# Routing without SyncE's waits for stores, and routing and experts in one block of the program

## The chip, the cores and the metric

The kernel runs on one core of one Trainium2 chip, in one launch. The metric is device time in microseconds (us): the median of three runs. One further execution was recorded by the hardware profiler, and all rows below come from it. TensorE is written PE, its weight load PEld, VectorE DVE, ScalarE ACT, GpSimd POOL, SyncE SP. A row of the engine "SPq" is a DMA that SP issued.

## The reference, cut to what matters

One decoder layer over 1024 tokens of width 1024, in float32. Attention and pooling come first; the change lies in the two stages after them.

```python
x = x + (sigmoid(g_a) * y_attn + sigmoid(g_p) * y_pool) @ W_o   # called x1 below
h = rmsnorm(x, g_ffn)                                           # called h2 below
logits = h @ w_router + b_router                                # 1024 tokens x 32 experts
top_val, top_idx = lax.top_k(logits, 4)
gates = softmax(top_val)
# tokens sorted by expert, in blocks; each block goes through its expert:
gu = xb @ w_gate_up[e] + b_gate_up[e]
act = (min(up) + 1) * gate * sigmoid(1.702 * gate)
y = act @ w_down[e] + b_down[e]
x = x + sum over a token's 4 experts of gate * y
```

## The kernel before

The program is a row of stages, each a block with one instruction stream per engine: front, attend, merge, route, experts, combine. Between two blocks stands a barrier: an engine that has ended its part of a block waits until all five have.

**Routing** (`route`, L1325 to L1736) makes x1 and h2 for 8 tiles of 128 tokens, numbered n = 0 to 7, in pairs p = 0 to 3 (tiles 2p and 2p + 1). PE multiplies the merged rows by W_o in seven products per pair (L1475, a Strassen scheme; order in `ORDER`), and between these matmuls, at fixed places (`between` in the PE part), does the router work for the pair before: `turn` (eight transposes of h2, L1484), `parts` (router product, L1495), `logits` (L1505) and `ranks` (L1513, L1514). After the last pair come the router steps of tiles 6 and 7 alone, with rows of idle transposes (`stay_warm`, L1518, and L1542). DVE adds the products and the input tile `xt` into `x1[b]`, b = n % 2 (L1611 is the first write into `x1[1]`, in `second_right`; L1638 and L1626 the last ones, for the even and the odd tile, which raise `x1_sum`), scales it to `h2[b]` (L1644, raises `h2_ready`), picks four experts (L1658 to L1665), and turns the ranks into places in the slot list (L1669 to L1688; L1672 raises `base`, for which the next `parts` on PE waits).

POOL makes the sums of input rows that the Strassen scheme needs (L220, four per pair, for the pair ahead), and for each tile writes 4 x 128 token numbers to the slot list in DRAM, by four indirect DMAs of 128 words each (`scatter`, L1403); it waits until they have landed before it goes on. Scatter n runs after DVE has placed tile n. The scatter of the last tile stands in the experts block (L1889). At its end POOL gathers the rows of the first expert item from DRAM (L1435, L1436).

SP issues per tile: the load of input tile n + 2 (L1367), the store of x1 (L1369) and the store of h2 (L1370), 512 KB each. Then it waits until both stores have landed and raises `rows_free`, for which `tile_free` on DVE waits before L1611 (odd tiles) and L1630 (even tiles) overwrite `x1[b]`. Its loop, and what DVE waits for:

```python
if n + 2 < T:
    sp.wait_ge(sem("x1_sum"), n + 1)
    sp.dma_start(xt[b], ...)                       # L1367
sp.wait_ge(sem("h2_ready"), n + 1)
sp.dma_start(x1_dram[rows, :], x1[b])              # L1369
sp.dma_start(h2_dram[rows, :], h2[b])              # L1370
sp.wait_ge(sem("stored"), 32 * n + 32)             # L1371
sp.sem_inc(sem("rows_free"), 1)                    # L1372
...
dve.wait_ge(xt_here[n % 2], 16 * (n // 2 + 1))     # tile_free
dve.wait_ge(sem("rows_free"), n + 1)
```

**Experts** (`experts`, L1750 on) works through items: 160 tokens of one expert, then narrower ones. PE transposes the gathered rows (`turn_x`, L1908, L1912), ACT copies them to SBUF (L2096 to L2099), PE multiplies by the expert's weights (L1927 and others), with DVE and ACT behind it. Before its first item, ACT makes the exponentials of the gates (L2167) and DVE the table of items (from L2402 on), which SP writes out and reads back (L1860, L1862). SP loads 12 MB of weights per item; half of the first item's gate and up weights are loaded at the start of route, the other half by `load_gate_up(sp, 0, 1)` (L1374, issued at L1287) as route's last act on SP, after the gathered rows are there.

Of the kernel before, what the change touches and what calls it, by code (L numbers as in the profile page):

```python
# [20 lines left out]
ALU = mybir.AluOpType  # L21
# [62 lines left out]
def build(nc, x, p, positions, g_mix, w_in, g_q_lat, w_q_b, g_kv_lat, w_kv_b, g_q_head, g_k_nope,  # L84
# [39 lines left out]
    with ExitStack() as top:  # L124
# [1199 lines left out]
        def route():  # L1324
            ctx, sem = stage("route")  # L1325
            with ctx:
                x1 = [view(arena_a, D * (2 + b), D) for b in (0, 1)]
                h2 = [view(arena_a, D * (4 + b), D) for b in (0, 1)]
                junk = view(arena_a, D * 6, D // 2).bitcast(BF16)
                h2T = [view(arena_h, D * (2 + b), K, P) for b in (0, 1)]  # L1330
                zeros = view(arena_h, 4608, SLOTS // P + 2).bitcast(I32)
                ms, rms, rstd = (view(arena_h, 5132 + j, 1) for j in range(3))
                logit = view(arena_h, 5152, E)
                top8 = view(arena_h, 5184, 8)
                idx8 = view(arena_h, 5192, 8).bitcast(U32)
                idxf = [view(arena_h, at, TOP_K) for at in (5200, 7360)]
                onehot = [view(arena_h, at, TOP_K, E) for at in (5248, 7232)]
                taken = view(arena_h, 5376, TOP_K, E)
                slot_e = view(arena_h, 5504, E)
                destf = view(arena_h, 5568, TOP_K)  # L1340
                partT = [view(arena_h, 6912 + P * b, P) for b in (0, 1)]
                fold = view(arena_h, 7168, E)
                QUADS = P // E
                found, place_of, hit = (view(arena_h, 6144 + 2 * P * j, 2 * P) for j in range(3))
                tokc, place, one = (view(arena_h, 4880 + j, 1) for j in range(3))
                earlier = sb("r_earlier", [P, P], BF16, ctx=ctx)
                ones = sb("r_ones", [P, P], BF16, ctx=ctx)
                chosen = [sb(f"r_chosen{b}", [P, E], BF16, ctx=ctx) for b in (0, 1)]
                TB0, TB1, LG, RK = banks[4:8]

                def parts_bank(n):

                    return OUT[1] if n == T - 1 else RK
                with nc.Block() as block:
                    @block.sync
                    def _(sp):
                        sp.wait_ge(sem("zeros"), 1)
                        sp.dma_start(list_dram.rearrange("(p s) o -> p (s o)", p=P), zeros).then_inc(sem("listed"), 16)

                        load_gate_up(sp, 0, 0)  # L1360
                        sp.sem_inc(sem("rows_free"), 2)
                        for n in range(T):
                            b = n % 2
                            rows = slice(tile_of(n) * P, (tile_of(n) + 1) * P)
                            if n + 2 < T:
                                sp.wait_ge(sem("x1_sum"), n + 1)
                                sp.dma_start(xt[b], x2d[tile_of(n + 2) * P:(tile_of(n + 2) + 1) * P, :]).then_inc(xt_here[b], 16)  # L1367
                            sp.wait_ge(sem("h2_ready"), n + 1)
                            sp.dma_start(x1_dram[rows, :], x1[b]).then_inc(sem("stored"), 16)  # L1369
                            sp.dma_start(h2_dram[rows, :], h2[b]).then_inc(sem("stored"), 16)  # L1370
                            sp.wait_ge(sem("stored"), 32 * n + 32)  # L1371
                            sp.sem_inc(sem("rows_free"), 1)  # L1372
                        sp.wait_ge(out_done, 7 * PAIRS)
                        sp.wait_ge(rows_here, 32)  # L1374
                        load_gate_up(sp, 0, 1)

                    @block.gpsimd
                    def _(pool):
                        pool.memset(zeros, 0).then_inc(sem("zeros"), 1)
                        pool.iota(tok, pattern=[[P, T]], base=0, channel_multiplier=1).then_inc(sem("consts"), 1)  # L1380
                        pool.iota(part, pattern=[[1, 1]], base=0, channel_multiplier=1,
                                  allow_small_or_imprecise_dtypes=True).then_inc(sem("consts"), 1)
                        pool.memset(ones[:, :], 1.0).then_inc(sem("consts"), 1)
                        pool.memset(found, 0.0).then_inc(sem("consts"), 1)
                        pool.iota(place_of[:, 0:P], pattern=[[1, P]], base=1, channel_multiplier=0,
                                  allow_small_or_imprecise_dtypes=True).then_inc(sem("consts"), 1)
                        pool.iota(place_of[:, P:2 * P], pattern=[[0, QUARTERS], [1, REST]], base=P + 1, channel_multiplier=0,
                                  allow_small_or_imprecise_dtypes=True).then_inc(sem("consts"), 1)
# [1266 lines left out]
```

## Time and profile before

| | us |
|---|---|
| median of three runs | 2417.8 |
| the three runs | 2417.48, 2417.8, 2420.49 |
| the profiled execution, its own time | 2423.67 |
| span of its trace, first to last instruction | 2422.1 |
| busy in the span: PE / DVE / ACT / POOL | 2371.3 / 1331.2 / 460.3 / 425.9 |
| mean granted TensorE clock | 0.993 |

The trace puts the route block from about 666 us to 808 us after the span's start, and the experts block after it. In rows of a timeline the columns are: start, busy time, engine, line, operation, output and input, count, and in brackets the engine's idle time before it with what ended it. "PEq L1354" and the like is the release of the barrier. Granted clock 1.00 is TensorE's 2.4 GHz, 0.50 is 1.2 GHz.

### The profile page before, as it was taken

The page shows a single profiled execution, that of the slowest core. Times are in us where ns is not written, and L with a number is a line of the kernel's source. Part 1 is how long each engine was busy: PE and PEld are TensorE (multiplying, and loading weights), DVE is VectorE, ACT ScalarE, POOL GpSimd, SP SyncE. Part 2 cuts the span into 40 slices and gives each one's busy share as a digit, 9 for nine tenths or more (in the row PEclk, how much of TensorE's full clock was granted, in tenths as well). Part 3 has the DMA queues.
Part 4 walks back from the last instruction along what each step waited for, and adds up shares of the span by engine and source line. Part 5 has one row for each costly group of instructions (what it writes and reads, how often), then busy time and mean ns, then how long its engine had stood idle before and what let it go on. Part 6 is the DMA issues. An engine that isn't in the chain of part 4 may idle for free. (4 is left out here: it accounts for less than half of the span.)

```text
span 2422.1 us, 45423 instructions
## 1 busy us (share of the span) xinstructions
PE 2371.3 (98%) x15700; PEld 1614.1 (67%) x15700; DVE 1331.2 (55%) x2477; ACT 460.3 (19%) x1150; POOL 425.9 (18%) x589
## 2 busy tenths in 40 slices
PE   8999999999998899999999999999999999999999
PEld 6765664444443888888888888887656565555544
DVE  4665674111255555444544554555767677676565
ACT  3334551000021100001000100000222212121332
POOL 2450102121333211000110110011010101111230
PEclk9999999999998899999999999999999999999999
DMA  4000002311052699887888888888999999999462
GB/s 150 27 18 10 1 0 53 122 29 49 28 176 70 221 377 324 297 294 281 301 294 301 289 308 312 315 301 305 339 329 357 340 345 342 342 347 336 168 200 87
DMA packets 255033, 531.84 MB, mean 220 GB/s; under 512 B 17845, under 2 KB 67909, under 8 KB 254950
## 3 DMA queue, kind: packets, MB, share of 16 engines
q1 hardware_dynamic: 222302, 472.57, 54.9%
q0 software_dynamic: 17440, 38.97, 5.2%
q10 hardware_dynamic: 15208, 19.14, 2.2%
q8 instruction: 58, 0.95, 0.2%
q14 instruction: 25, 0.20, 0.0%
HBM read 498.76 MB, written 31.87 MB: 219 GB/s over the span
## 5 line engine op out<-in xcount | busy, mean ns | idle before, releaser
L1927 PEld LDWEIGHTS banks<-arena_a,arena_w 128*128 128x128 f32 x4608 | 562.9, 190 | 8.1 <-issue 6.5
L1927 PE MATMUL banks<-arena_a,arena_w 128*128 128x144 f32 (+7 forms) x4608 | 566.7, 286 | 1.4 <-ACT arena_a L2099 1.4
L1980 PE MATMUL banks<-arena_w,arena_a 128*64 128x256 f32 x2688 | 298.6, 380 | 3.0 <-DVE arena_a L2258 1.7
L1980 PEld LDWEIGHTS banks<-arena_w,arena_a 128*64 128x64 f32 x2688 | 193.3, 137 | 107.3 <-issue 14.1
L2353 DVE TENSOR_SCALAR arena_m<-banks,arena_m 128x160 f32<-128x160 f32 x144 | 55.2, 383 | 297.1 <-PE banks L1927 296.6
L1305 POOL DMA_DIRECT2D arena_m<-slot_tokens x32 | 18.8, 587 | 1025.7 <-issue 1025.7
L2154 ACT ACTIVATE arena_m<-arena_m 128x160 f32<-128x160 f32 x144 | 48.5, 337 | 785.7 <-DVE arena_m L2353 472.7
L1935 PE MATMUL banks<-arena_w,arena_a 128*64 128x256 f32 x1728 | 197.5, 381 | 0.0
L2036 PE MATMUL banks<-arena_w,arena_a 128*128 128x512 f32 x448 | 194.6, 592 | 0.0
L1935 PEld LDWEIGHTS banks<-arena_w,arena_a 128*64 128x64 f32 x1728 | 120.9, 137 | 67.6 <-issue 10.4
L2036 PEld LDWEIGHTS banks<-arena_w,arena_a 128*128 128x128 f32 x448 | 84.0, 190 | 100.4 <-issue 100.4
L2601 PE MATMUL banks<-arena_h,arena_w 128*128 128x512 f32 (+1 forms) x272 | 111.2, 567 | 0.0
L1129 PE MATMUL banks<-arena_a,arena_w 128*128 128x512 f32 x224 | 97.3, 592 | 0.0
L2601 PEld LDWEIGHTS banks<-arena_h,arena_w 128*128 128x128 f32 x272 | 51.1, 190 | 55.3 <-issue 54.5
L1129 PEld LDWEIGHTS banks<-arena_a,arena_w 128*128 128x128 f32 x224 | 42.6, 190 | 53.6 <-issue 53.6
L285 PE MATMUL banks<-arena_m 96*128 96x512 f32 (+2 forms) x192 | 76.8, 509 | 1.0 <-PEq L366 1.0
L2276 DVE TENSOR_TENSOR arena_w<-arena_w 128x2048 f32<-128x2048 f32 x28 | 64.2, 2292 | 18.9 <-PE banks L1980 17.3
L1104 PE MATMUL banks<-arena_h,arena_w 128*128 128x512 f32 x168 | 74.4, 592 | 0.0
L2279 DVE TENSOR_TENSOR arena_w<-arena_w 128x2048 f32<-128x2048 f32 x28 | 64.2, 2293 | 17.2 <-PE banks L1980 15.0
L293 DVE TENSOR_REDUCE arena_w<-banks 128x1 f32<-128x128 f32 (+3 forms) x64 | 48.4, 757 | 44.3 <-PE banks L288 43.9
L2117 ACT ACTIVATE ex_more<-banks 128x256 f32<-128x256 f32 x28 | 10.8, 384 | 300.5 <-PE banks L1980 300.5
L1307 POOL DMA_DIRECT2D arena_m<-slot_tokens x128 | 66.4, 524 | 3.8 <-issue 3.0
(410 smaller groups left out, 3451.9 us busy)
## 6 DMA issues: line engine op xcount, KB each, us to landing
arena_w<-in_w_gate_up_dram SPq DMA_DIRECT2D x128, 2048.0 KB, 12.7
arena_w<-in_w_down_dram SPq DMA_DIRECT2D x32, 4096.0 KB
expert_rows<-arena_a ACTq DMA_DIRECT2D x104, 128.0 KB, 8.7
arena_a<-in_x_dram SPq DMA_DIRECT2D x16, 512.0 KB, 4.6
arena_w<-in_w_in_dram SPq DMA_DIRECT2D x16, 512.0 KB, 5.4
arena_a<-in_b_down_dram SPq DMA_DIRECT2D x14, 512.0 KB, 15.3
expert_rows<-arena_a ACTq DMA_DIRECT2D x28, 192.0 KB
arena_a<-in_b_down_dram SPq DMA_DIRECT2D x72, 64.0 KB
```

Source lines behind the costliest of these rows:

```text
L285: m = pe.matmul(score[s % 2][j // BANK][:, 0:w], qTh[b][0:HD, s * P:(s + 1) * P], kTh[b][0:HD, j:j + w], start=True, stop=not last, skip_g ...
L1104: m = pe.matmul(bank[:, :], w[:, k, :], src[:, k, :], start=(start and k == 0), stop=(stop and k == KH - 1), skip_group_check=True)
L1129: m = pe.matmul(bank[:, :], w[b][:, k, :], src[:, k, half], start=(k == 0), stop=(k == kk - 1))
L1307: pool.dma_start(idx_b[q * REST:(q + 1) * REST, :], list_dram[bass.ds(slot + P, REST), :]).then_inc(rows_listed, 16)
L1927: m = pe.matmul(GU[f % 3][:, to:to + width], w[c][:, k, at:at + P], xT[:, k, 0:width], start=(k == 0), stop=(k == K - 1), skip_group_check ...
L1935: m = pe.matmul(at[h * TH:(h + 1) * TH, :], x[:, k, :], w[:, k, h * QB:(h + 1) * QB], start=(start and k == 0), stop=(stop and k == KH - 1 ...
L1980: m = pe.matmul(at[h * TH:(h + 1) * TH, :], x[:, k, :], w[:, k, h * QB:(h + 1) * QB], start=(start and k == 0), stop=(stop and k == KH - 1 ...
L2036: return pe.matmul(DN[j][:, :], actT[:, k, 0:P], wd[:, k, halves[j]], start=(k == 0), stop=(k == KF - 1))
L2276: dve.tensor_tensor(b11, b12, b11, ALU.add).then_inc(sem("w_sums"), 1)
L2279: dve.tensor_tensor(b21, b21, b11, ALU.subtract).then_inc(sem("w_sums"), 1)
L2353: dve.tensor_scalar(gc[f % 2], bank[:, 0:WIDTH], bias[:, f:f + 1], SWIGLU_LIMIT, ALU.add, ALU.min).then_inc(sem("gc"), 1)
L2601: m = pe.matmul(gate_into(n, j, part), xnT[n % 2][:, k, :], w_gate[:, k, part], start=(k == 0), stop=(k == K - 1))
```

## The change

SP no longer waits for stores. Each of the two `x1[b]`/`h2[b]` buffers has a semaphore of its own, `stored0` and `stored1`, and DVE waits for it directly. The store of x1 moves from behind `h2_ready` to behind `x1_sum`. `route` and `experts` put their parts into one block; POOL, whose next part begins with the last tile's scatter, gets a wait for that tile's places. The rest of the diff, some 2,000 lines, is indentation; without it:

```diff
-        def route():
-            ctx, sem = stage("route")
-            with ctx:
+        def route(block, ctx, sem):
...
-                with nc.Block() as block:
                     @block.sync
                     def _(sp):
...
                         load_gate_up(sp, 0, 0)
-                        sp.sem_inc(sem("rows_free"), 2)
                         for n in range(T):
                             b = n % 2
                             rows = slice(tile_of(n) * P, (tile_of(n) + 1) * P)
-                            if n + 2 < T:
-                                sp.wait_ge(sem("x1_sum"), n + 1)
+                            sp.wait_ge(sem("x1_sum"), n + 1)
+                            if n + 2 < T:
                                 sp.dma_start(xt[b], x2d[...]).then_inc(xt_here[b], 16)
+                            sp.dma_start(x1_dram[rows, :], x1[b]).then_inc(sem(f"stored{b}"), 16)
                             sp.wait_ge(sem("h2_ready"), n + 1)
-                            sp.dma_start(x1_dram[rows, :], x1[b]).then_inc(sem("stored"), 16)
-                            sp.dma_start(h2_dram[rows, :], h2[b]).then_inc(sem("stored"), 16)
-                            sp.wait_ge(sem("stored"), 32 * n + 32)
-                            sp.sem_inc(sem("rows_free"), 1)
+                            sp.dma_start(h2_dram[rows, :], h2[b]).then_inc(sem(f"stored{b}"), 16)
...
-                        pool.wait_ge(sem("stored"), 32 * T)
+                        pool.wait_ge(sem("stored0"), 32 * (T // 2))
+                        pool.wait_ge(sem("stored1"), 32 * (T // 2))
...
                         def tile_free(n):
                             dve.wait_ge(xt_here[n % 2], 16 * (n // 2 + 1))
-                            dve.wait_ge(sem("rows_free"), n + 1)
+                            if n >= 2:
+                                dve.wait_ge(sem(f"stored{n % 2}"), 32 * (n // 2))
...
-        def experts():
-            ctx, sem = stage("ex")
-            with ctx:
+        def experts(block, ctx, sem, route_sem):
...
-                with nc.Block() as block:
...
                     @block.gpsimd
                     def _(pool):
+                        pool.wait_ge(route_sem("dst"), T)
                         pool.tensor_copy(tokb[1], tok[:, T - 1:T]).then_inc(sem("tokb"), 1)
...
-        route()
-        experts()
+        route_ctx, route_sem = stage("route")
+        experts_ctx, experts_sem = stage("ex")
+        with route_ctx, experts_ctx:
+            with nc.Block() as block:
+                route(block, route_ctx, route_sem)
+                experts(block, experts_ctx, experts_sem, route_sem)
         combine()
```

SP's stream in the routing loop, the turns of tiles 1 and 2, before (the names after "waits" are semaphores; x_rows and h_rows are the x1 and h2 arrays in DRAM):

```order
L1367 DMA arena_a<-in_x_dram 128x1024 [waits route_stored,route_x1_sum]
L1369 DMA x_rows<-arena_a 128x1024 [waits route_h2_ready]
L1370 DMA h_rows<-arena_a 128x1024
L1367 DMA arena_a<-in_x_dram 128x1024 [waits route_stored,route_x1_sum]
L1369 DMA x_rows<-arena_a 128x1024 [waits route_h2_ready]
L1370 DMA h_rows<-arena_a 128x1024
```

And with the change:

```order
L1364 DMA arena_a<-in_x_dram 128x1024 [waits route_x1_sum]
L1365 DMA x_rows<-arena_a 128x1024
L1367 DMA h_rows<-arena_a 128x1024 [waits route_h2_ready]
L1364 DMA arena_a<-in_x_dram 128x1024 [waits route_x1_sum]
L1365 DMA x_rows<-arena_a 128x1024
L1367 DMA h_rows<-arena_a 128x1024 [waits route_h2_ready]
```

The wait for `stored` is gone from SP, and the x1 store stands in front of the wait for `h2_ready`.

POOL's stream where routing ends and experts begin, as one piece of the difference:

```order
-L1435 DMA arena_a<-h_rows,arena_m 128x1024 [waits idx_here,route_stored]
-L1436 DMA arena_a<-h_rows,arena_m 128x256
-L1354 UNCONDITIONAL_BRANCH
-L1884 UNCONDITIONAL_BRANCH [waits barrier_Pool_Activation_PE_DVE_SP_gather]
-L1886 COPY arena_h<-arena_h 128x1
+L1431 DMA arena_a<-h_rows,arena_m 128x1024 [waits idx_here,route_stored1,route_stored0]
+L1432 DMA arena_a<-h_rows,arena_m 128x256
+L1879 UNCONDITIONAL_BRANCH
+L1882 COPY arena_h<-arena_h 128x1 [waits route_dst]
```

The barrier's wait is gone; the copy that starts the last scatter waits for `dst` in its place. On PE, ACT, DVE and SP the same place loses the one branch with its wait for the barrier and nothing else moves.

## Rows read from the trace of the kernel before

**Rows 1.** The page's busy time of PE, with its share of the span
```profile
PE 2371.3 (98%) x15700; PEld 1614.1 (67%) x15700; DVE 1331.2 (55%) x2477; ACT 460.3 (19%) x1150; POOL 425.9 (18%) x589
```

**Rows 2.** Waits of SP, 640 to 850 us: line, releaser, total, times, longest
```profile
SPq L1372 <- DMA h_rows<-arena_a: 33.7, 5, 10.4
```

**Rows 3.** Timeline of PE in route: first matmul of `parts` and of `ranks`, pairs 1 to 3
```profile
698.24 0.64 PE L1495 MATMUL banks<-arena_h 128*32 128x128 f32 x16 [0.17 <-DVE arena_h L1672]
...
705.15 0.18 PE L1513 MATMUL banks<-r_chosen,r_earlier 128*128 128x32 bf16 x1
...
731.55 1.08 PE L1495 MATMUL banks<-arena_h 128*32 128x128 f32 x16 [5.20 <-DVE arena_h L1672]
...
741.47 0.18 PE L1513 MATMUL banks<-r_chosen,r_earlier 128*128 128x32 bf16 x1
...
766.13 1.08 PE L1495 MATMUL banks<-arena_h 128*32 128x128 f32 x16 [3.12 <-DVE arena_h L1672]
...
775.82 0.18 PE L1513 MATMUL banks<-r_chosen,r_earlier 128*128 128x32 bf16 x1
```

**Rows 4.** Timeline of DVE in pairs 2 and 3
```profile
711.17 0.68 DVE L1626 TENSOR_TENSOR arena_a<-banks,arena_a 128x512 f32<-128x512 f32 x1
...
713.59 1.28 DVE L1644 SCALAR_TENSOR_TENSOR arena_a<-arena_a,arena_h,gain_row 128x1024 f32<-128x1024 f32 x1
...
721.14 0.68 DVE L1603 TENSOR_TENSOR arena_a<-banks,arena_a 128x512 f32<-128x512 f32 x1
728.69 0.69 DVE L1611 TENSOR_TENSOR arena_a<-arena_a 128x512 f32<-128x512 f32 x1 [6.87 <-SPq L1372]
...
763.61 0.69 DVE L1611 TENSOR_TENSOR arena_a<-arena_a 128x512 f32<-128x512 f32 x1 [5.34 <-SPq L1372]
```

**Rows 5.** Timeline of the DMAs that SP issues in pairs 2 and 3
```profile
716.80 0.33 SPq L1367 DMA_DIRECT2D arena_a<-in_x_dram  x1
...
717.66 0.43 SPq L1370 DMA_DIRECT2D h_rows<-arena_a  x1
...
752.84 0.33 SPq L1367 DMA_DIRECT2D arena_a<-in_x_dram  x1
```

**Rows 6.** Windows: length, busy time per engine, granted clock, DMA share, GB/s
```profile
724.00:726.00 2.00, 2.00 (x8) 0.72 (x6) 0.00 (x0) 0.00 (x0) 0.00 (x0) 1.00 0.07 10
...
732.00:734.00 2.00, 2.00 (x14) 1.02 (x7) 1.79 (x7) 0.28 (x1) 0.18 (x1) 0.50 0.00 0
```

**Rows 7.** Timeline of POOL: a scatter's first issue, and what followed scatters 1, 3, 4
```profile
715.70 0.98 POOL L1403 DMA_INDIRECT slot_tokens<-arena_h  x1 [0.78 <-POOL arena_h L1399]
...
728.87 1.63 POOL L220 TENSOR_TENSOR arena_h<-arena_m 128x512 f32<-128x512 f32 x1 [8.36 <-DMA slot_tokens<-arena_h]
...
763.44 0.19 POOL L1399 COPY arena_h<-arena_h 128x1 int32<-128x1 int32 x1 [9.12 <-DMA slot_tokens<-arena_h]
...
778.33 0.19 POOL L1399 COPY arena_h<-arena_h 128x1 int32<-128x1 int32 x1 [4.93 <-DMA slot_tokens<-arena_h]
...
794.59 0.99 POOL L1403 DMA_INDIRECT slot_tokens<-arena_h  x1 [0.86 <-DVE arena_h L1688]
```

**Rows 8.** Timeline of all engines where route ends and experts begins
```profile
800.60 7.21 PE L1542 MATMUL banks<-ident 128*128 128x128 f32 x40
...
803.24 0.97 POOL L1436 DMA_INDIRECT arena_a<-h_rows,arena_m  x1 [0.30 <-issue]
807.37 1.01 SPq L1287 DMA_DIRECT2D arena_w<-in_w_gate_up_dram  x2
808.82 1.28 ACT L2167 ACT_TABLE_LOAD   x1 [13.35 <-PEq L1354]
...
809.01 0.41 PE L1908 MATMUL banks<-ident,arena_a 128*128 128x128 f32 x2 [1.20 <-PEq L1354]
```

**Rows 9.** Waits of POOL, 660 to 840 us: line, releaser, total, times, longest
```profile
POOL slot_tokens L1403 <- DVE arena_h L1688: 9.5, 4, 4.9
```

**Rows 10.** All issues of the scatters' line: count, ns shortest, median, longest
```profile
L1403 POOL DMA_INDIRECT slot_tokens<-arena_h x28: 962/972/1948, 702.5 to 798.4; - x28
```

1898 lines of the change are left out of this document (949 added, 949 removed).

## The prediction

> **What bounds the kernel now.** The page first: PE is busy 98% of the span [rows 1], so a change outside PE's work can only win back the rest: idle time of PE, and time in which PE works at the lower clock. The waits of SP show what the change takes away there: 33.7 us in five waits for stores [rows 2]. SP is no bound, so the question is who waits for what SP does late. DVE does. In pair 2 its last sum before the wait ends at 721.14 + 0.68 = 721.82, and L1611 starts at 728.69, 6.87 us later, released by SP's `rows_free`; in pair 3 it waits 5.34 us for the same [rows 4]. And PE waits for DVE: the `parts` of the odd tile needs `base`, which DVE raises 2.9 us after its release (728.69 to 731.55) in pair 2 and 2.5 us after it (763.61 to 766.13) in pair 3. PE stands still 0.17, 5.20 and 3.12 us there in pairs 1, 2 and 3 [rows 3]. After the stall of pair 2 the window from 732 us shows a granted clock of 0.50, that is 1.2 GHz, with PE fully busy [rows 6]. Its price can be read off: from the first `parts` matmul to the first `ranks` matmul PE has the same work in each pair, and takes 705.15 - 698.24 = 6.9 us in pair 1 but 741.47 - 731.55 = 9.9 us in pair 2 and 775.82 - 766.13 = 9.7 us in pair 3 [rows 3]. So each stall costs its own length and about 3 us more. Last I read the place where the blocks meet [rows 8]. No other wait of PE in this stretch is touched by the diff.
>
> **Stores and loads issued earlier.** In pair 2 the stores of tile 3 must land before L1611. Before, the load of tile 5 goes out at 716.80, because SP waits for tile 2's stores, and the h2 store of tile 3 at 717.66 [rows 5]. With the change SP issues the load and the x1 store when `x1_sum` comes, at 711.17 + 0.68 = 711.85, and the h2 store when `h2_ready` comes, at 713.59 + 1.28 = 714.87 [rows 4]: 4.9 us earlier for 1 MB of the three transfers and 2.8 us for the last 0.5 MB. How much earlier they land, no row shows, so I bound it. If the landing moves only as far as the last issue, DVE is released 2.8 us earlier, at 725.9. At the other end it doesn't wait at all, 721.8. Between: the first 1.5 MB (tile 4's load, tile 2's stores) were down when SP went on at 716.80; the next 1.5 MB needed until about 724, when the DMA rate has fallen to 10 GB/s [rows 6], that is some 6.5 us from the issue, of which I estimate 2 us to be start-up that a queue which never runs empty doesn't pay. Following directly on the first part they end near 721, with landing near 722.5. PE was ready at 731.55 - 5.20 = 726.35 and needs DVE released 2.9 us before, by 723.5. I take the middle value, since it rests on how long the same bytes moved: the stall of **5.2 us** goes, and with it the low clock's **3.0 us**.
>
> In pair 3 the load of tile 7 waits in the same way, until 752.84 [rows 5], and the threshold is nearer: PE was ready at 766.13 - 3.12 = 763.01, so DVE must be released by 760.5, 3.1 us earlier than it was. The last issue alone gives 2.8 us of that, the shorter queue the rest. I count the stall, **3.1 us**, and the clock's **2.8 us** as gone, with less confidence. In pair 1 there are only 0.17 us to win. What is late next there is PE's own work: with the stalls gone PE issues its matmuls without a pause until the end of pair 3.
>
> **The first of those to be late after that: POOL.** POOL waits for each scatter's landing. From the last issue's end that took 4.93 us for scatter 4, which runs alone, but 8.36 and 9.12 us for scatters 1 and 3, beside the loads and stores [rows 7]. From 728.87 to the first issue of scatter 6 at 794.59 are 65.7 us. In these POOL waited for DVE up to 9.5 us [rows 9], so its own chain is about 56.2 us, waits for PE's products included, which shrink with the stalls. PE and DVE reach that place 5.2 + 3.0 + 3.1 + 2.8 = 14.1 us sooner, at 780.5. POOL, if scatter 1 lands 2 us sooner than at 728.9, gets there at 726.9 + 56.2 = 783.1 at the latest. That gives back between nothing and 2.6 us; because of the waits still inside the chain I take **1.0 us**. The sums of rows for PE (L220) are not late: they are made a pair ahead, and PE never waited for one here.
>
> **No barrier between the blocks.** SP issues two loads after the gathered rows have landed, at 807.37, for 1.01 us; only then does the barrier open, and PE starts its transposes at 809.01, 1.20 us after its idle transposes ended (800.60 + 7.21 = 807.81) [rows 8]. Now PE waits for the rows alone, which were there before 807.37: **1.2 us**. ACT loads its table at 808.82 for 1.28 us, to 810.10 [rows 8], and only then copies what PE transposed. With no barrier it loads it while it idles (13.35 us before). Bounds: nothing, and 810.10 - 809.01 = 1.1 us; PE needs most of that for the first bank of transposes, so I take **0.3 us**. DVE's table of items starts some 7 us sooner, which pays nothing: PE has the first item's matmuls to do meanwhile, and the table's DMAs stand behind 4 MB of weights in SP's queue. The last scatter moves up behind the gather; it costs nothing, since POOL's next use of the list waits for the table anyway. The cost of `rows_free` and of POOL's new wait for `dst` is nil: both are conditions already true.
>
> One thing speaks against the earlier start of DVE. Issues of scatters take 972 ns in the median and up to 1948 ns [rows 10], the long ones beside DVE work. The Trainium skill says why in "SBUF — State Buffer", section "SBUF: two separate sides": VectorE in its two-port modes locks GpSimd out of their shared port, and descriptors of a GpSimd DMA can't be written meanwhile. By that rule the two gathers, the second issued at 803.24 [rows 8], would now meet DVE's table work, where before DVE idled. From rows alone: two issues lengthened by 0.98 us each is 2.0 us, the high bound; nothing is the low one. DVE's first table operations are as short as routing's, beside which most issues took the median, so I take nothing.
>
> **The sum**: -5.2 - 3.0 - 3.1 - 2.8 + 1.0 - 1.2 - 0.3 = -14.6 us. The experts stage is PE's own work from there on, so it moves up as a whole. Against the profiled execution's 2423.67 us this is 2409.1. The median of the runs lies 5.9 us below that execution; I apply the same difference to it: 2417.8 - 14.6 = **2403.2 us**.
>
> **The rivals.**
> *The stores still land late.* For it: in pair 2 the DMA engines had all but stopped by 724 to 726 us [rows 6], yet DVE was released at 728.69 [rows 4] and POOL, for its scatter, at 728.87 [rows 7]. So the release came with the scatter's last word, not with the stores' data. If that coupling is the limit, only the 2.8 us of the later issue are won in each pair, PE still stalls 2.4 and 0.3 us, and one of the two low-clock stretches stays at most times: -2.8 - 2.8 - 1.5 = -7.1 us with both low clocks kept, 2410.7, and -10.0 with one gone, 2407.8. Against it: the h2 store now enters the queue at 714.87, before scatter 1's first issue at 715.70 [rows 7]. The Trainium skill has such a coupling in "DMA: Bandwidth & Descriptors", section "Queues, rings and completion order": a semaphore's increment lands only after every earlier write of that DMA engine, across its queues. By that rule tile 3's stores escape the scatter if their data get ahead of it, and don't where they queue behind it. The rows of pair 2 agree with it, but no row tells which comes first in the new order. Chance 0.27. In the same band falls the case that the stalls are partly the profiler's, since the plain runs are 5.9 us shorter.
> *The DMA engines are the limit*, and the same bytes land at the same time whatever the issue order. Then only the joint gains: -1.5 us, 2416.3. Against it: 10 GB/s in a window just before the release. Chance 0.12.
> *Slower, by POOL's scatters.* Now loads and stores of two tiles may be queued when a scatter comes, and each scatter's landing takes longer. POOL's chain has four landings before scatter 6, so it grows fourfold; the kernel is slower than before from 726.9 + chain > 794.59 + 1.5, a chain of 69.2 us, that is from 3.3 us more per scatter. The step from alone to beside stores was 9.12 - 4.93 = 4.2 us. With 5 us more on each, scatter 6 starts at 726.9 + 76.2 = 803.1, 8.5 us later than before: 2417.8 + 8.5 - 1.5 = 2424.8. Against it: the bytes are the same and start earlier, so they are more often gone when the scatter comes. Chance 0.06.
>
> **How the numbers follow.** The forecast has 0.55; its own range, from the table load's and the tail's bounds and the clock's, is 2400 to 2406. The range of 8 in 10 takes the late-landing rival in and reaches up to where "same" begins, 2400 to 2413. A measurement of this kernel tells 0.2%, 4.8 us, from no change. Forecast and first rival are faster by more than that (0.82), the second within it (0.12), the third slower (0.06).
>
> **What the profile would show.** Right: no wait of DVE's L1608 (L1611 before) above 2 us; PE's wait before `parts` in pairs 2 and 3 under 0.5 us, and the `parts` to `ranks` stretch 6.9 us in all pairs at clock 1.00; PE's first expert transposes directly behind its idle ones; ACT's table load before the gathered rows land. Wrong: a DVE wait for `stored1` of 3 us or more ending together with POOL's wait for its scatter; or POOL's first issue of scatter 6 waiting for a landing, not for DVE.

## The result, and the profile after

The changed kernel took 2408.5 us (median of five runs, 2406.92 to 2410.38), and the kernel before, run beside it, 2420.5 us: a ratio of 0.995 with a 95% interval of 0.9938 to 0.9961. So it is faster, by 12.0 us. The forecast was 2403.2 us in a range of 2400 to 2413, and 14.6 us to be won. The five runs of before are the three from which the forecast was drawn and two more (2421.43 and 2421.52 us); with these the median is 2.7 us above the 2417.8 of the forecast, and the rest of the miss, 2.6 us, is in the sum. The profiled execution took 2410.38 us (before 2423.67), span 2408.7 us. All shifts below are taken against `ranks` of pair 1, which the change hardly touches (PE's wait in pair 1 was 0.17 us) and which stands 0.37 us later than before (705.52 against 705.15 [rows 3]). Each run has such a small shift of its own; where times of two runs are set against each other below, it is taken off.

PE in route, timeline of the kernel after, the rows that answer to [rows 3] (the line is L1491 now, and L1509 for `ranks`):

```profile
698.62 0.65 PE L1491 MATMUL banks<-arena_h 128*32 128x128 f32 x16
...
705.52 0.18 PE L1509 MATMUL banks<-r_chosen,r_earlier 128*128 128x32 bf16 x1
...
728.13 0.64 PE L1491 MATMUL banks<-arena_h 128*32 128x128 f32 x16 [1.40 <-DVE arena_h L1669]
...
735.04 0.18 PE L1509 MATMUL banks<-r_chosen,r_earlier 128*128 128x32 bf16 x1
...
757.79 0.64 PE L1491 MATMUL banks<-arena_h 128*32 128x128 f32 x16 [1.54 <-DVE arena_h L1669]
...
764.70 0.18 PE L1509 MATMUL banks<-r_chosen,r_earlier 128*128 128x32 bf16 x1
```

The stalls of 5.20 and 3.12 us have shrunk to 1.40 and 1.54, they are not gone. From `parts` to `ranks` it is 6.91 us in both pairs, as in pair 1: the low clock behind each stall is gone whole.

DVE's first write into `x1[1]` (L1608 now), SP's issues of pair 2, and POOL's scatters around them, timelines of the kernel after, for [rows 4], [rows 5] and [rows 7]:

```profile
725.61 0.69 DVE L1608 TENSOR_TENSOR arena_a<-arena_a 128x512 f32<-128x512 f32 x1 [3.61 <-DMA h_rows<-arena_a]
...
755.27 0.69 DVE L1608 TENSOR_TENSOR arena_a<-arena_a 128x512 f32<-128x512 f32 x1 [3.76 <-DMA h_rows<-arena_a]
```
```profile
711.99 0.33 SPq L1364 DMA_DIRECT2D arena_a<-in_x_dram  x1
712.37 0.71 SPq L1365 DMA_DIRECT2D x_rows<-arena_a  x1
715.02 0.32 SPq L1367 DMA_DIRECT2D h_rows<-arena_a  x1
```
```profile
717.02 0.98 POOL L1398 DMA_INDIRECT slot_tokens<-arena_h  x1 [0.78 <-POOL arena_h L1394]
...
728.38 1.27 POOL L220 TENSOR_TENSOR arena_h<-arena_m 128x512 f32<-128x512 f32 x1 [6.54 <-DMA slot_tokens<-arena_h]
...
783.62 0.98 POOL L1398 DMA_INDIRECT slot_tokens<-arena_h  x1 [1.76 <-DVE arena_h L1685]
```

The issues came as early as worked out (load of tile 5 at 711.99, h2 store at 715.02), yet the landing came at 725.6, not 722.5. Windows of the kernel after in that stretch (columns as in [rows 6]):

```profile
718.00:720.00 2.00, 2.00 (x8) 1.00 (x7) 0.30 (x2) 0.28 (x1) 1.39 (x3) 1.00 1.03 422
720.00:722.00 2.00, 2.00 (x11) 1.23 (x10) 1.86 (x8) 0.00 (x0) 1.53 (x2) 1.00 0.47 177
722.00:724.00 2.00, 2.00 (x8) 1.04 (x7) 0.00 (x0) 1.09 (x2) 0.00 (x0) 1.00 0.01 0
```

The DMA engines are full to 720 and empty by about 721, and then DVE waits 4.7 us more for a store whose bytes have gone by. These empty microseconds are what the experiments are about.

The joint, timeline of the kernel after, for [rows 8]:

```profile
784.22 1.28 ACT L2163 ACT_TABLE_LOAD   x1
...
789.34 6.49 PE L1538 MATMUL banks<-ident 128*128 128x128 f32 x40
...
796.65 0.44 PE L1904 MATMUL banks<-ident,arena_a 128*128 128x128 f32 x2 [0.83 <-DMA arena_a<-h_rows,arena_m]
...
798.98 13.31 PE L1923 MATMUL banks<-arena_a,arena_w 128*128 128x160 f32 x96 [1.01 <-ACT arena_a L2095]
```

PE waits for the gathered rows now, not for the barrier, and ACT loads its table 12 us before it is needed.

### The profile page after: what moved, and what is told of

It reads as the page before. It is cut to its first block and busy times, and to the rows that moved or that the text cites. A ratio compares the mean times of both kernels' runs of the same rounds, so it can differ in the third digit from the quotient of the medians.

```text
span 2408.7 us, 45402 instructions
## 1 busy us (share of the span) xinstructions
PE 2364.5 (98%) x15700; PEld 1611.2 (67%) x15700; DVE 1334.0 (55%) x2477; ACT 460.3 (19%) x1150; POOL 423.7 (18%) x589
```

## The experiments

Two theories for what is left of DVE's wait. **Coupling**: a store's completion is held up while list writes (POOL's scatter, 512 writes of 4 bytes per tile) are in flight. **Bytes**: the loads and stores just take that long. Each kernel ran five to eleven times, on chips on which before took 2424 to 2426 us, so only the ratios are compared; "ratio" is to the kernel before on the same chip, with its 95% interval. Diffs are against the changed kernel unless said.

**Each half of the change alone.** First SP's half in the two blocks of before (diff against the kernel before):

```diff
+                            sp.dma_start(x1_dram[rows, :], x1[b]).then_inc(sem(f"stored{b}"), 16)
                             sp.wait_ge(sem("h2_ready"), n + 1)
...
-                            sp.wait_ge(sem("stored"), 32 * n + 32)
-                            sp.sem_inc(sem("rows_free"), 1)
...
-                            dve.wait_ge(sem("rows_free"), n + 1)
+                            if n >= 2:
+                                dve.wait_ge(sem(f"stored{n % 2}"), 32 * (n // 2))
```

> The change's SP edit alone, route and experts as two blocks with the barrier between them. Theory (two parts that add up, as the change's profile reads: the stalls and the low clock in pairs 2 and 3 give some 11.4 us, the missing barrier some 1.4 us): 1.4 us slower than the change, ratio to the kernel before about 0.9957; PE waits 1.4 and 1.5 us before parts of tiles 3 and 5, no window at clock 0.50 between 730 and 772 us, PE's first expert transposes again behind a barrier release. Rival (the parts depend on each other, since the barrier hid or took over what the stalls cost): over 4 us slower than the change.

Measured: ratio 0.9966 (0.9954 to 0.9978), 2414.3 against 2424.3 us. DVE waits 4.29 and 4.42 us, PE 2.07 and 2.20, and there is no low clock behind them. By the ratio it is 3.9 us slower than the change, where 1.4 was expected. The barrier's cost is there as before, and here more than its wait: a stretch of low clock follows (in the kernel before the clock is full there), and the first item's matmuls take 36.72 us, in the change 35.04 (timeline of PE, then a window):

```profile
789.39 6.55 PE L1540 MATMUL banks<-ident 128*128 128x128 f32 x40
797.31 0.41 PE L1907 MATMUL banks<-ident,arena_a 128*128 128x128 f32 x2 [1.37 <-PEq L1354]
...
799.94 36.72 PE L1926 MATMUL banks<-arena_a,arena_w 128*128 128x160 f32 x256 [1.35 <-ACT arena_a L2098]
```
```profile
801.00:803.00 2.00, 2.00 (x10) 2.00 (x9) 1.93 (x4) 0.19 (x1) 1.70 (x2) 0.50 1.05 392
```

Then the one block with SP's part as it was:

```diff
-                    sp.wait_ge(sem("x1_sum"), n + 1)
                     if n + 2 < T:
+                        sp.wait_ge(sem("x1_sum"), n + 1)
...
+                    sp.wait_ge(sem("stored"), 32 * n + 32)
+                    sp.sem_inc(sem("rows_free"), 1)
```

> One block for route and experts, SP's waits for stores and rows_free as before. Theory of two parts that add up: 1.4 us faster than before, ratio about 0.9994; PE still waits about 5.2 and 3.1 us before parts of tiles 3 and 5 and works at clock 0.50 for 6.8 us after each; its expert transposes follow the idle ones as in the change. Rival (DVE's early start on the item table and the last scatter, moved behind the gathers, make the gathered rows land later, so the joint is worth nothing): within 0.3 us of before, with PE's wait for the gathered rows over 2 us.

Measured: ratio 0.9986 (0.9977 to 0.9995), 2421.6 us. PE stands still 5.55 and 4.28 us, and the low clock follows both times:

```profile
731.00:733.00 2.00, 2.00 (x10) 0.84 (x3) 1.82 (x8) 0.28 (x1) 0.00 (x0) 0.50 0.00 0
767.00:769.00 2.00, 2.00 (x4) 0.72 (x3) 0.31 (x3) 0.00 (x0) 1.10 (x2) 0.50 0.00 0
```

(windows of this run). The two halves, 0.34% and 0.14%, add up to the change's 0.5% within their intervals, and SP's half is the larger. The intervals reach 2 to 3 us to each side, so these times leave room for an interplay of a microsecond or two, such as the low clock behind the barrier in e1.

**List writes taken away beside the stores.** This kernel leaves out the list writes of tiles 1 and 3 (`SKIP` is 1, 3), so those tiles' tokens are missing from the slot list; all else runs:

```diff
-                    for j in range(TOP_K):
+                    for j in range(0 if n in SKIP else TOP_K):
```

> The change, with the list writes (four indirect DMAs each) of tiles 1 and 3 left out; those tokens' entries in the slot list stay zero, so their experts' rows are token 0's. Amount of work elsewhere is the same. Theory A (the stores' semaphores are held by the scatter's writes to DRAM): DVE's waits at L1608 in pairs 2 and 3 fall from 3.6 and 3.8 us to under 0.5, PE's 1.4 and 1.5 us to nothing, 2.9 us faster than the change. Theory B (the bytes of two tiles' loads and stores set the landing, at some 400 GB/s): DVE's waits stay between 3 and 4 us and the time within 0.5 us of the change.

Measured: ratio 0.9924 (0.991 to 0.9937), 2405.5 us. Timelines of DVE and PE, and two windows:

```profile
720.86 0.69 DVE L1609 TENSOR_TENSOR arena_a<-arena_a 128x512 f32<-128x512 f32 x1 [0.66 <-DMA h_rows<-arena_a]
```
```profile
718.00:720.00 2.00, 2.00 (x9) 1.04 (x8) 1.83 (x9) 0.00 (x0) 0.00 (x0) 1.00 0.80 326
720.00:722.00 2.00, 2.00 (x9) 1.11 (x8) 0.90 (x2) 1.09 (x2) 0.00 (x0) 1.00 0.03 10
```

The same store, the same bytes before it: the engines run empty at about 719.6 (0.80 of the first window), and DVE goes on at 720.9, 1.3 us after that; in the change it was 725.6 - 720.9 = 4.7 us (0.47 of the window from 720). On the change's scale, 1.8 us later (`ranks` of pair 1 at 703.74 here), the landing would be 722.6. DVE waits 0.66 us instead of 3.61. PE has no wait before `parts` at all. Coupling holds; bytes are excluded as the cause of 3 of these 4.7 us. Pair 3 shows the same: in the change the engines run empty at about 750.5 and DVE goes on at 755.27, again 4.7 us later, and without the list writes DVE doesn't wait there. Since tokens are missing, the ratio of this kernel is no gain to be had. The Trainium skill's rule in "DMA: Bandwidth & Descriptors", section "Queues, rings and completion order", is that the semaphore's increment lands only after every earlier write of that DMA engine, whatever its queue; this trace agrees.

**The list writes held instead of left out.** A first try named the wrong count, and POOL waited for stores that had landed long before:

```diff
+                    if n in (1, 3):
+                        pool.wait_ge(sem("stored1"), 16 * (n + 1))
```

> The change, with the list writes of tiles 1 and 3 held back on POOL until both stores of that tile have landed. Coupling theory: with no list write in flight the stores land at about 721 us, as they did where the list writes were left out, DVE's waits at L1608 are under 1 us in both pairs and PE's at parts nothing (2.9 us won), while POOL's chain grows by some 2 to 4 us per hold and gives that back at the gathers: about the change's time, up to 3 us slower. Bytes theory: DVE's waits stay at 3.6 us and POOL's holds come on top.

Measured: ratio 0.9947 (0.9933 to 0.996), DVE waits 4.11 and 3.20 us, PE 1.88 and 0.98. It held nothing, so it is a second measurement of the change, and shows how far two traces of one kernel differ: half a microsecond in each of these waits, and 0.6 us at the first expert matmul. With the count of the stores meant:

```diff
-                        pool.wait_ge(sem("stored1"), 16 * (n + 1))
+                        pool.wait_ge(sem("stored1"), 16 * (n + 3))
```

> The hold of the run before was put on stores that had landed 20 us earlier: scatter 1 runs beside tile 3's stores, not tile 1's. Here the list writes of tile 1 wait until tile 3's stores have landed, those of tile 3 until tile 5's have; nothing is left out. Coupling theory: DVE's waits at its first write into x1[1] fall from 3.6 and 3.8 us to under 1 us, as without those list writes, and PE's waits at parts vanish; POOL's chain grows by about 4 us per hold (scatter 1 from 717 to 721 us, after that list writes with no stores beside them), so the gathers come 2 to 6 us later and the whole is 0 to 4 us slower than the change. Bytes theory: DVE's waits stay at 3.6 us.

Measured: ratio 0.9972 (0.9961 to 0.9983), 2418.0 us. Timelines of POOL, DVE and PE:

```profile
720.73 1.06 POOL L1400 DMA_INDIRECT slot_tokens<-arena_h  x1 [6.26 <-DMA h_rows<-arena_a]
...
788.25 0.98 POOL L1400 DMA_INDIRECT slot_tokens<-arena_h  x1 [0.78 <-POOL arena_h L1394]
```
```profile
751.83 1.31 DVE L1610 TENSOR_TENSOR arena_a<-arena_a 128x512 f32<-128x512 f32 x1 [2.54 <-DMA h_rows<-arena_a]
```
```profile
800.53 0.56 PE L1906 MATMUL banks<-ident,arena_a 128*128 128x128 f32 x2 [4.65 <-DMA arena_a<-h_rows,arena_m]
```

With no list write in flight the stores of tile 3, the last of them issued at 713.24, land by 720.7, and in pair 2 DVE doesn't wait. In pair 3 it does, for 2.54 us, where under 1 was expected. The hold had pushed scatter 2 among the next transfers: its four issues went out from 736.07 to 741.83, the loads and stores of tiles 4 and 5 from 736.71 to 743.37. In that stretch the DMA engines were busy and moved little (window of this run):

```profile
742.00:744.00 2.00, 2.00 (x6) 0.75 (x4) 1.30 (x2) 1.28 (x3) 0.00 (x0) 1.00 1.24 162
```

They ran empty at about 750.8, and DVE went on 1.1 us after that, so this wait was for late data and not for a late completion. The rest of the time is lost behind: POOL's chain is some 6 us late, scatter 6 starts at 788.25 and waits for a landing, PE waits 4.65 us for the gathered rows, and with the low clock behind that wait the first item's matmuls take 36.87 us instead of 35.04. By the ratios the kernel is 5.3 us slower than the change; 0 to 4 was expected. That is the slower rival's mechanism, made by hand.

**The x1 store's place.** Behind `h2_ready`, as before:

```diff
-                    sp.dma_start(x1_dram[rows, :], x1[b])...
                     sp.wait_ge(sem("h2_ready"), n + 1)
+                    sp.dma_start(x1_dram[rows, :], x1[b])...
```

> The change with the x1 store moved back behind the wait for h2_ready. Coupling theory (what counts is which store data get ahead of the list writes): two stores, not one, now go out at 715.0 us, 2 us before scatter 1's first issue, so the h2 store is further back in the queue and DVE's waits grow by up to 1 us, PE's with them: 0 to 2 us slower than the change. Rival (the early x1 store is what the gain came from): the waits return to 5 us and more and a window at clock 0.50 follows, over 5 us slower than the change.

Measured: ratio 0.9942 (0.9928 to 0.9956). DVE waits 3.61 and 4.91 us, PE 1.43 and 2.69. The times show no difference from the change, so the earlier x1 store is not where the bulk of the gain came from. The one trace shows some: a low clock follows the stall of 2.69 us, and the first expert matmul comes 2.5 us later than in the change, more than the 0.6 us by which two traces of the change differ.

**DVE waits only for what it overwrites.** L1608 writes `x1`, not `h2`, so a semaphore for each store lets it start when the x1 store alone has landed; the wait for the h2 store moves to where `h2[b]` is written:

```diff
-                        dve.wait_ge(sem(f"stored{n % 2}"), 32 * (n // 2))
+                        dve.wait_ge(sem(f"x1_out{n % 2}"), 16 * (n // 2))
...
+                    if n >= 2:
+                        dve.wait_ge(sem(f"h2_out{n % 2}"), 16 * (n // 2))
```

> The change, with x1's and h2's stores on semaphores of their own: DVE waits for x1's store before it overwrites x1, and for h2's store only before it overwrites h2, some 20 us later. Both theories let the x1 store, issued 4.6 us before the first list write of scatter 1, land before DVE wants it at 722 us: DVE's waits at its first write into x1[1] under 0.5 us, PE's 1.4 and 1.5 us gone, 2.9 us faster than the change, ratio to before about 0.9939. Rival (x1's semaphore too is held by scatter 0's or 1's writes, or the wait turns up at h2's scaling): a DVE wait of 2 us or more at one of the two places, and less than 1 us gained.

Measured: ratio 0.995 (0.9937 to 0.9964), 2411.8 us: no gain over the change (0.9939 was expected), though in pairs 2 and 3 neither DVE nor PE waits at these places any more. Timelines of POOL and PE:

```profile
781.48 0.26 POOL L1394 COPY arena_h<-arena_h 128x1 int32<-128x1 int32 x1 [4.96 <-DMA slot_tokens<-arena_h]
782.52 0.99 POOL L1398 DMA_INDIRECT slot_tokens<-arena_h  x1 [0.78 <-POOL arena_h L1394]
```
```profile
783.15 7.24 PE L1538 MATMUL banks<-ident 128*128 128x128 f32 x40
795.10 0.44 PE L1906 MATMUL banks<-ident,arena_a 128*128 128x128 f32 x2 [4.71 <-DMA arena_a<-h_rows,arena_m]
798.13 37.07 PE L1925 MATMUL banks<-arena_a,arena_w 128*128 128x160 f32 x256 [0.96 <-ACT arena_a L2097]
```

What was won in route is waited away at its end: POOL is the late one there now, and behind the 4.71 us the clock falls to 0.50 (window 797 to 800), so the first item's matmuls take 37.07 us where they take 35.04 in the change.

**Gather first.** The scatter of tile 6 moved behind the two gathers, with and without the split semaphores:

```diff
-                scatter(T - 2, last=True)
...
                 pool.indirect_dma_start(xq, None, h2_quarters, ...)
+                scatter(T - 2, last=True)
```

> Split semaphores, and POOL issues the two gathers of the first item before the list writes of tile 6 instead of behind them (the gathers take their rows from PE's own search, not from the list). Theory (with the stalls gone POOL's chain of list writes reached the gathers last: scatter 6 was issued at 782.5 us, on scatter 5's landing, the gathers behind it, and PE waited 4.7 us for the rows, which brought the low clock back): PE's wait for the rows under 0.5 us, no clock of 0.50 behind the idle transposes, 4.7 us for the wait and 2 us for the clock less than the split alone, ratio to before about 0.9922. Rival (the gathered rows are late for another cause, h2's stores or the gathers' own reads beside list writes): PE still waits over 2 us and the ratio stays near 0.995.

> The change with the gathers ahead of tile 6's list writes and nothing else. In the change POOL waited for DVE there and PE waited 0.83 us for the rows, so by the theory that POOL's chain is hidden in the change there are 0.8 us to win, ratio about 0.9947 if the change is 0.995, with DVE's waits at L1608 still near 3.6 us. Rival (the list writes' traffic beside the gathers costs more than their place in the queue): the rows come no earlier.

Measured: 0.9947 (0.9933 to 0.996) with the split, 0.9971 (0.9962 to 0.998) without, which is worse than the change. Neither is what was expected (0.9922 and 0.9947). The rows do come in time: PE waits 0.29 us for them with the split and not at all without. But (timelines of PE, with the split and then without it)

```profile
791.36 17.65 PE L1924 MATMUL banks<-arena_a,arena_w 128*128 128x160 f32 x128 [1.02 <-ACT arena_a L2093]
...
813.90 20.56 PE L1924 MATMUL banks<-arena_a,arena_w 128*128 128x160 f32 x128 [4.89 <-DMA arena_w<-in_w_gate_up_dram]
```
```profile
822.21 20.05 PE L1922 MATMUL banks<-arena_a,arena_w 128*128 128x160 f32 x128 [4.10 <-DMA arena_w<-in_w_gate_up_dram]
```

the half of the first item's weights that is loaded late, now with the list writes of two tiles beside it, isn't there when PE asks for it, and 128 matmuls at partly low clock take 20.56 us instead of 17.65. From its first issue (789.06 with the split, 797.49 without) it takes 24.8 and 24.7 us; in the change (796.68) PE needs it after some 20 us and doesn't wait. Some 10 us after that issue the DMA engines are as busy as in the change and move far less (a window with the split, then one of the change):

```profile
799.00:801.00 2.00, 2.00 (x17) 2.00 (x16) 0.65 (x3) 0.23 (x1) 0.00 (x0) 1.00 0.93 150
```
```profile
807.00:809.00 2.00, 2.00 (x17) 2.00 (x16) 0.99 (x4) 0.34 (x1) 0.00 (x0) 1.00 1.06 399
```

The wait moved once more. These rows point to the list writes as the cause, but no run leaves them out at this place, so it is not shown.

**More list writes in flight.** Split semaphores, and POOL no longer waits for a scatter's landing before its next work, so two tiles' list writes can be on their way:

```diff
+                    if n >= 2:
+                        pool.wait_ge(scattered[b], 64 * (n // 2))
                     pool.tensor_copy(tokb[b], tok[:, tile_of(n):tile_of(n) + 1])
...
-                    if not last:
-                        pool.wait_ge(scattered, 64 * n + 64)
-                        pool.sem_inc(sem("dst_free"), 1)
...
-                    dve.wait_ge(sem("dst_free"), n + 1)
+                    if n >= 2:
+                        dve.wait_ge(scattered[b], 64 * (n // 2))
```

> Split semaphores, and POOL no longer waits for a tile's list writes before it goes on: even and odd tiles' list writes have semaphores of their own, POOL waits for those of tile n - 2 before it reuses their buffer, DVE waits for them directly. Theory (with the stalls gone, POOL's chain of landings is what the gathers wait for): scatter 6's first issue follows DVE's places at about 778 us instead of 782.5, gathers issued at about 784, PE's wait for the rows falls from 4.7 us to under 1 us, no 0.50 clock behind the idle transposes: 6.7 us under the split alone, ratio to before about 0.9922. Rival (the list writes are limited in DRAM at some 2 us per DMA, so that more of them in flight only queue, and hold the stores, h2's landing and the gathered rows as before): PE's wait for the rows stays over 3 us and the ratio near 0.995.

Measured: ratio 0.9949 (0.9936 to 0.9963), where 0.9922 was expected. The wait for the gathered rows is gone and the clock is full there, as expected, but PE waits 2.42 and 3.50 us before `parts`. Timelines of POOL and DVE:

```profile
707.73 0.98 POOL L1401 DMA_INDIRECT slot_tokens<-arena_h  x1 [0.90 <-DVE arena_h L1687]
```
```profile
723.62 1.37 DVE L1607 TENSOR_TENSOR arena_a<-arena_a 128x512 f32<-128x512 f32 x1 [3.96 <-DMA x_rows<-arena_a]
...
755.91 0.69 DVE L1607 TENSOR_TENSOR arena_a<-arena_a 128x512 f32<-128x512 f32 x1 [5.71 <-DMA x_rows<-arena_a]
```

Scatter 1 starts 7.0 us earlier than in the change (717.02, less 2.3 us of shift): its list writes are issued while SP issues the transfers (706.03 to 712.69 here), and no longer behind them. Now even the x1 stores are late, for which DVE had not waited at all in the run with the split alone. DMA issues from 700 to 815 us, first of the split alone, then of this run (count, KB each, median us to landing):

```profile
arena_a<-in_x_dram SPq DMA_DIRECT2D x4, 512.0 KB, 6.8
```
```profile
arena_a<-in_x_dram SPq DMA_DIRECT2D x4, 512.0 KB, 13.2
```

The loads of input tiles take 13.2 us instead of 6.8. This is another effect than the held completion. Windows of this run:

```profile
716.00:718.00 2.00, 2.00 (x7) 0.98 (x6) 0.60 (x4) 0.00 (x0) 0.00 (x0) 1.00 1.04 84
...
722.00:724.00 2.00, 2.00 (x8) 0.76 (x6) 0.38 (x1) 0.00 (x0) 1.85 (x2) 1.00 0.22 57
```

The DMA engines are busy but move 84 GB/s, where the change, just as busy, moves 422 (its window from 718). They run empty at about 722.4, and DVE goes on 1.2 us after that, as it does without list writes (e3, 1.3 us). So list writes issued together with the transfers make their data late, as in pair 3 of e9; list writes issued behind them, while their data move, make only the completion late.

**Only the last scatters overlapped.** As e4, but of POOL's waits for a landing only the one between tile 5's and tile 6's list writes is taken away; DVE waits directly for the landing out of the buffer of places that it overwrites:

```diff
-                    if not last:
-                        pool.wait_ge(scattered, 64 * n + 64)
+                    if n < T - 3:
+                        pool.wait_ge(scattered[b], 64 * (n // 2 + 1))
```

> Split semaphores for the x1 and h2 stores, as in e4_split_semaphores, and one more thing: POOL no longer waits for the landing of tile 5's list writes before it starts those of tile 6 (each of the two buffers of places has its own semaphore, and DVE waits for the one that it overwrites). If POOL's chain of landings is what held the gathered rows back in e4, scatter 6's first issue comes near 777.5 us instead of 782.5, the gathers near 784, PE's wait for the gathered rows falls from 4.7 us to under 1, there is no low clock behind the idle transposes, and the ratio is near 0.992. Rival: the list writes themselves are slow where they land, so that two tiles' writes in flight take as long as one after the other; then scatter 6 is issued early but the gathered rows are still 3 us or more late, and the ratio stays near 0.995.

Measured: ratio 0.993 (0.9917 to 0.9944), 2408.1 against 2425.3 us. Timelines of POOL and PE:

```profile
777.96 0.99 POOL L1399 DMA_INDIRECT slot_tokens<-arena_h  x1 [3.83 <-DVE arena_h L1687]
...
786.18 0.99 POOL L1430 DMA_INDIRECT arena_a<-h_rows,arena_m  x1 [3.40 <-DVE arena_m L1682]
```
```profile
703.58 0.18 PE L1508 MATMUL banks<-r_chosen,r_earlier 128*128 128x32 bf16 x1
...
792.16 0.44 PE L1908 MATMUL banks<-ident,arena_a 128*128 128x128 f32 x2 [0.87 <-DMA arena_a<-h_rows,arena_m]
794.49 35.04 PE L1927 MATMUL banks<-arena_a,arena_w 128*128 128x160 f32 x256 [1.01 <-ACT arena_a L2099]
```

As expected: scatter 6 waits for DVE, not for a landing, the wait for the gathered rows is 0.87 us, and the window 790 to 800 has clock 1.00. Only the gathers come 2 us later than I wrote (DVE is the late one for them). Against `ranks` of pair 1 (703.58 here, 705.52 in the change) the first expert matmul comes 798.98 - 794.49 - 1.94 = 2.55 us earlier than in the change. That is the best complete version of these runs; its interval still touches that of the change, so its lead rests on the trace as much as on the times.

## Why the prediction came out as it did

The forecast's own range was 2400 to 2406 us, and 2408.5 is outside it; it is inside the wider range because that took in the first rival, with 2410.7 us, or 2407.8 with one low clock gone. What came lies between the two: the rival's late landing, with the forecast's full clock.

*Stall of pair 2, -5.2*: 5.20 to 1.40, so -3.8. *Stall of pair 3, -3.1*: 3.12 to 1.54, so -1.6. These two terms were too large, by 2.9 us together, and the step that failed in both is "landing near 722.5": I took the middle value from how long the bytes move. The bytes did move by about 721, as worked out; but completion is not the end of the bytes, and came at 725.6. Without list writes it would have come at 722.6, so the working held for the stores alone; scatter 1 is what it left out (e3, e9). The prediction had named this as its first rival, and half of its sign appeared: "a DVE wait for `stored1` of 3 us or more" did, "ending together with POOL's wait" did not. DVE went on at 725.61, POOL at 728.38, so the stores wait for a part of the list writes, not for the last. Which part isn't settled. The threshold in PE did the rest: of DVE's 3.61 us only 1.40 reach PE.

*Low clock, -3.0 and -2.8*: both gone, -3.0 and -2.8. Here the rival was too dark; a stall of 1.4 or 1.5 us was followed by none, one of 5.55 or 4.28 by one each (e2). Between, e6, e7 and e10 have one behind 3.64, 2.69 and 3.50 us, but none behind 1.91, 1.43 and 2.42. In these cases a stall of half the length thus cost a good deal less than half.

*POOL, +1.0*: nothing was given back. In the change scatter 6 waits 1.76 us for DVE. I had POOL 1 us behind DVE and it was about 1 us ahead (0.78 of the 1.76 us pass before a scatter even where nothing is late, as before scatter 1), in part because DVE was later than forecast. The margin is thin: as soon as the two stalls are gone (e4), POOL's landing is last, as this term feared.

*Barrier, -1.2*: the wait at the joint went from 1.20 to 0.83 us, a gain of only 0.4. That the rows "were there before 807.37" was right, but the idle transposes ended at 807.81, so the rows were only 0.4 us ahead of PE, and the gathers, which wait for DVE and POOL and not for the barrier, came no earlier by its going. The rows also took 3.7 us from the end of the second gather's issue (792.97 to 796.65), before at most 3.2 (804.21 to 807.37); why was not tried. In its place the idle transposes took 6.49 us instead of 7.21 [rows 8], 0.7 us. Together -1.1, the right number for a half wrong reason. *Table load, -0.3*: PE's wait for ACT fell by 0.3 us, from 1.35 in the kernel before to 1.01.

*The port.* No loss, as taken: the two gathers took 1.00 and 0.97 us to issue beside DVE's small table operations. The last scatter's second and third issue, beside DVE operations on 128x1024 elements, took 1.66 and 1.30 us, and PE waits for none of them.

The measured terms give -3.8 - 3.0 - 1.6 - 2.8 - 1.1 - 0.3 = -12.6; the profiled executions differ by 13.3 and the medians by 12.0. That the sum of 14.6 is only 1.3 us off the profiled executions is in part luck: the 2.9 us too much for the stalls stand against the 1.0 us for POOL that was not given back. The rest of the 5.3 us between 2403.2 and 2408.5, 4.0 us, is none of the kernel's: I carried 5.9 us of difference between the profiled execution and the median over to the changed kernel, where it is 1.9.

## What to carry to other kernels

A store's bytes and its completion are two times: where a wait for a DMA ends in a stretch in which the DMA engines stand empty, look for small writes of another queue in flight before you make room for bytes. Moving those writes is no sure cure: held back they made the chain behind them late (e9), issued earlier, together with the transfers, they made the data late (e10). What paid was to wait for less. Let an engine wait for the one transfer whose buffer it overwrites, not for a pair. And when a stall goes, the wait reappears at the next joint that was nearly late (here POOL's landings, then the gathered rows, then the weights), so take out the next one in the same step: e4 alone won nothing over the change, with e11's edit its trace is 2.55 us ahead of the change's.

## What was unexpected of the hardware

Four list writes of 128 words keep a store of another queue from completing for 3 us and more after its data have moved: from the engines running empty to DVE's release it took 4.7 us with them and 1.3 us without (e3); from the h2 store's issue it was 725.61 - 715.02 = 10.6 us with them, and in e9, where they are held back, at most 720.73 - 713.24 = 7.5 us. Issued together with the loads and stores they doubled the median landing of the loads, from 6.8 to 13.2 us, and the busy DMA engines moved 84 GB/s instead of 422 (e10).

And PE's clock: in the tail of route the granted clock is low in the change as well. The window of the kernel after reads

```profile
783.00:793.00 10.00, 6.24 (x41) 5.60 (x42) 6.78 (x44) 1.79 (x3) 5.89 (x7) 0.50 0.11 10
```

and only the last of the idle transposes run at full clock. PE had eight short waits from 767 us to 789, of 0.5 to 1.9 us, most of them for DVE and ACT in the router steps of the last tiles. What that costs, and whether more idle transposes there would pay, was not tried.
